# A three-block transformer kernel: the changes of sub-layer reordered, operands moved to equal addresses modulo 512, and another block order in the second-last weight unit

## The reference

```python
# first block, each with its own shift, scale, gate: x = x + c*(1 + gate) * rms_norm(f(h), post)
h = rms_norm(x, pre) * (1 + scale) + shift
f = swiglu, then hybrid_mixer (spatial gating beside forgetting attention), then swiglu
# second block: x = x + c * rmsnorm(f(rmsnorm(x, pre)), post)
f = swiglu, then hybrid_mixer_2 (RWKV-7 recurrence beside a convolution), then swiglu
# third block, twice, no post norm: x = x + f(rms_norm_3(x, g))
f = mixer (sparse attention beside differential attention), then swiglu
# at the end
return rms_norm_3(x, g_final)
```

## Time and profile before

| | |
|---|---|
| median of 3 runs | 3654.48 us (3650.88 to 3655.13) |
| the profiled execution, its own time | 3657.05 us |
| its span from first to last instruction | 3655.3 us |
| TensorE busy with matmuls | 3482.2 us (95%) |
| VectorE busy | 1837.7 us (50%) |
| ScalarE busy | 1152.5 us (32%) |
| moved by DMA | 330.29 MB, mean 90 GB/s |

### The profile page before, as it was taken

The page is one execution under the profiler, slowest core; times in us unless marked ns, Lnnn a source line. Parts: engine busy times, 40 slices in busy tenths (PEclk is TensorE's granted clock), DMA queues, the critical chain, the costliest instruction groups (busy, mean ns, idle before and its releaser), DMA issues.

```text
span 3655.3 us, 47516 instructions
## 1 busy us (share of the span) xinstructions
PE 3482.2 (95%) x19430; PEld 2770.4 (76%) x19436; DVE 1837.7 (50%) x2690; ACT 1152.5 (32%) x1728; POOL 162.7 (4%) x136
## 2 busy tenths in 40 slices
PE   9999899899999999998799999999999999899999
PEld 7887776678887888767588888666888886578887
DVE  6667535522334223798742225796422358952233
ACT  2222434422223222442342224335322233442222
POOL 0000000000000000000000001330000022200000
PEclk7999999999999999999999999999999999999999
DMA  6455221122222222220022222110222221112222
GB/s 245 178 182 196 81 95 47 58 81 92 92 92 88 100 94 92 81 79 15 8 87 92 96 98 94 70 69 24 81 93 100 95 93 70 47 53 92 92 93 81
DMA packets 47846, 330.29 MB, mean 90 GB/s; under 512 B 5312, under 2 KB 5568, under 8 KB 9280
## 3 DMA queue, kind: packets, MB, share of 16 engines
q1 hardware_dynamic: 41216, 290.09, 22.0%
q0 software_dynamic: 6464, 37.80, 2.8%
HBM read 325.77 MB, written 2.10 MB: 90 GB/s over the span
## 4 chain that ended last, share of the span: by engine, by line
PE 81%; DVE 13%; ACT 3%; issue 1%; DMA 0%; SPq 0%; DVEq 0%; ACTq 0%
PE PS L2136 24%; PE PS L2138 24%; PE PS L2137 24%; DVE WL L2640 2%; PE PS L319 1%; DVE A L1148 1%; DVE M L1147 1%; ACT WH L2435 1%; PE PS L394 1%; DVE X L2775 1%; PE PS L376 1%; PE PS L324 1%; PE PS L1493 1%; PE PS L931 1%; DVE A L2748 1%
## 5 line engine op out<-in xcount | busy, mean ns | idle before, releaser
L2640 DVE TENSOR_TENSOR WL<-RAW,WH 128x2048 fp32r<-128x2048 f32 x264 | 613.7, 2324 | 309.0 <-ACT WH L2435 308.6
L2136 PE MATMUL PS<-EH,WH 128*128 128x512 f32 (+1 forms) x1536 | 584.4, 380 | 28.9 <-DVE EL L2806 11.5
L2136 PE MATMUL PS<-HH,WH 128*128 128x512 f32 (+1 forms) x1456 | 556.0, 382 | 47.7 <-DVE HL L2806 23.4
L2137 PE MATMUL PS<-EL,WH 128*128 128x512 f32 (+1 forms) x1536 | 581.1, 378 | 0.0
L2138 PE MATMUL PS<-EH,WL 128*128 128x512 f32 (+1 forms) x1536 | 580.9, 378 | 0.0
L2435 ACT ACTIVATE WH<-RAW 128x2048 fp32r<-128x2048 f32 x264 | 503.9, 1909 | 191.6 <-PE PS L2138 183.5
L2137 PE MATMUL PS<-HL,WH 128*128 128x512 f32 (+1 forms) x1456 | 546.8, 376 | 0.0
L2138 PE MATMUL PS<-HH,WL 128*128 128x512 f32 (+1 forms) x1456 | 546.2, 375 | 0.0
L2679 DVE TENSOR_TENSOR A<-SG,PS 128x512 f32 (+1 forms) x132 | 90.7, 687 | 807.6 <-ACT SG L2565 807.6
L2565 ACT ACTIVATE SG<-PS 128x512 f32<-128x512 f32 x132 | 78.8, 597 | 1099.3 <-PE PS L2138 1099.3
L2136 PE MATMUL PS<-WH,AH 128*128 128x512 f32 x1056 | 417.7, 396 | 0.3 <-DVE CV L2868 0.3
(11 more groups left out here) (417 smaller groups left out, 3798.8 us busy)
## 6 DMA issues: line engine op xcount, KB each, us to landing
RAW<-in_w SPq DMA_DIRECT2D x264, 1024.0 KB, 4.8
E<-in_ada POOLq DMA_DIRECT2D x28, 1024.0 KB, 5.0
E<-in_ada SPq DMA_DIRECT2D x4, 1024.0 KB, 11.7
G<-in_ada SPq DMA_DIRECT2D x4, 1024.0 KB, 20.4
X<-in_x SPq DMA_DIRECT2D x1, 2048.0 KB, 13.9
X<-in_xn POOLq DMA_DIRECT2D x1, 2048.0 KB, 11.5
out_x<-A SPq DMA_DIRECT2D x4, 512.0 KB, 2.8
R<-in_row_ffn_post POOLq DMA_DIRECT2D x4, 256.0 KB, 3.1
```

The costliest lines, as they stand in the source:

```text
L2136: nc.tensor.matmul(out, wh, xh, start=start, stop=False)
L2137: nc.tensor.matmul(out, wh, xl, start=False, stop=False)
L2640: nc.vector.tensor_tensor(WL[:, w % 2, :], RAW[:, w % 2, :], WH[:, w % 2, :].bitcast(F32), ALU.subtract).then_inc(w_lo, 1)
```

## The change

It has four edits.

1. The spacer `LINE` is 40 floats long instead of 8, so everything behind it (EH, E, HH, G, AH, AL, ST and the smaller tensors) starts 128 bytes later in each partition: at 128 modulo 512, like X, WH, WL, A and ONES.
2. `leave`: the blocks of the second-last unit go 3, 2, 0, 1 instead of 3, 0, 1, 2, among those of the last unit.
3. ScalarE and VectorE take their steps at a change of sub-layer in another order: the high and low halves of tokens 0 to 255 come before the additions of blocks 2 and 3 to X, and the scaling of tokens 2 and 3 moves from VectorE to ScalarE (`scaled`), with a semaphore `root_ready`.
4. The Newton step takes two operations behind the root instead of three (four after a post norm); the factor -0.5 goes into the mean. `square_out(i)` waits for the squares of the block before.

```diff
-        sb("LINE", [P, 8])
+        sb("LINE", [P, 40])
...
                 one(0, 3)
+                one(0, 2)
                 one(0, 0)
                 second_arrives()
                 one(1, 0)
-                one(0, 1)
+                one(0, 1).then_inc(w_used, 1)
                 one(1, 1)
-                one(0, 2).then_inc(w_used, 1)
                 one(1, 2)
...
                 def square_out(i):
+                    if i:
+                        act.wait_ge(sqh_done, t("sqh") + 2 * i)
...
+                def scaled(i):
+                    act.wait_ge(root_ready, t.add("root_ready"))
+                    nc.scalar.activation(HG[:, i, :], XT[:, i, :], ACT.Copy, scale=stat(i, 6)).then_inc(xs_done, 1)
+
+                for i in (0, 1):
+                    if post:
+                        square_out(i)
+                        root_out(i)
+                    square_in(i)
...
+                    split(last_w)
+                    if post:
+                        square_out(2)
+                    for n in range(4):
+                        hi(n)
+                    if post:
+                        square_out(3)
+                    else:
+                        square_in(2)
+                    split(last_w + 1)
+                    for n in range(4, KD):
+                        hi(n)
+                    if post:
+                        root_out(2)
+                        root_out(3)
+                        square_in(2)
+                    else:
+                        square_in(3)
+                    scaled(2)
+                    if post:
+                        square_in(3)
+                    scaled(3)
                     for n in range(KD, 2 * KD):
                         hi(n)
...
+                def newton(i, r):
+
+                    dve.wait_ge(root_begun, t.add("roots"))
+                    chain(nc.vector.tensor_scalar(stat(i, 5), r, r, stat(i, 4), ALU.mult, ALU.mult))
+                    return nc.vector.tensor_scalar(stat(i, 6), stat(i, 5), 1.5, r, ALU.add, ALU.mult)
...
-                    dve.wait_ge(root_begun, t.add("roots"))
-                    chain(nc.vector.scalar_tensor_tensor(stat(i, 4), stat(i, 0), 1.0 / D, stat(i, 2), ALU.mult, ALU.add))
-                    i_[0] = i
-                    root = newton(stat(i, 4), stat(i, 3))
+                    chain(nc.vector.scalar_tensor_tensor(stat(i, 4), stat(i, 0), 1.0, stat(i, 1), ALU.mult, ALU.add))
+                    chain(nc.vector.tensor_scalar(stat(i, 4), stat(i, 4), -0.5 / D, -0.5 * EPS, ALU.mult, ALU.add))
+                    chain(newton(i, stat(i, 3)))
...
                     dve.wait_ge(sqx_done, t("sqx") + i + 1)
-                    chain(nc.vector.tensor_scalar(stat(i, 10), stat(i, 8), 1.0 / D, EPS, ALU.mult, ALU.add))
-                    dve.wait_ge(root_begun, t.add("roots"))
-                    i_[0] = i
-                    root = newton(stat(i, 10), stat(i, 9))
+                    chain(nc.vector.tensor_scalar(stat(i, 4), stat(i, 8), -0.5 / D, -0.5 * EPS, ALU.mult, ALU.add))
+                    root = newton(i, stat(i, 9))
+                    if onward and i >= 2:
+                        root.then_inc(root_ready, 1)
+                        return
+                    chain(root)
...
+                    leaves = gained if post else add_out
                     split(last_w)
+                    leaves(2)
+                    for n in range(4):
+                        lo(n)
+                    leaves(3)
+                    for n in range(4, KD):
+                        lo(n)
+                    if not post:
+                        normed(2)
+                    split(last_w + 1)
                     if post:
                         add_out(2)
...
+                        add_out(3)
+                        normed(2)
                     normed(3)
                     for n in range(KD, 2 * KD):
                         lo(n)
```

More of the change, by code:

```diff
@@ L190, in build_program @@
         sqh_done, hg_done, sqx_done, xs_done, turned = (sem(n) for n in ("sqh_done", "hg_done", "sqx_done", "xs_done", "turned"))
-        root_begun, y_shifted = sem("root_begun"), sem("y_shifted")
+        root_begun, root_ready, y_shifted = sem("root_begun"), sem("root_ready"), sem("y_shifted")
         xn_loaded, gains_loaded, gains_made, gains_ready = (sem(n) for n in ("xn_loaded", "gains_loaded", "gains_made", "gains_ready"))
@@ L2520, in boundary @@
                 else:
[L2521 to L2524, removed]
+                    split(last_w)
[3 more added lines that the diff above has]
+                        hi(n)
                     if post:
                         square_out(3)
-                        root_out(3)
[L2528 to L2532, removed]
+                    else:
[5 more added lines that the diff above has]
+                        root_out(2)
+                        root_out(3)
+                        square_in(2)
+                    else:
+                        square_in(3)
+                    scaled(2)
                     if post:
-                        square_in(2)
-                    square_in(3)
+                        square_in(3)
+                    scaled(3)
                     for n in range(KD, 2 * KD):
@@ L2774, in add_out @@
                     dve.wait_ge(hg_done, t("hg") + 2 * i + 2)
-                    nc.vector.scalar_tensor_tensor(XT[:, i, :], HG[:, i, :], root, XT[:, i, :], ALU.mult, ALU.add).then_inc(x_done, 1)
+                    nc.vector.scalar_tensor_tensor(XT[:, i, :], HG[:, i, :], stat(i, 6), XT[:, i, :], ALU.mult, ALU.add).then_inc(x_done, 1)
                 def normed(i):
                     dve.wait_ge(sqx_done, t("sqx") + i + 1)
-                    chain(nc.vector.tensor_scalar(stat(i, 10), stat(i, 8), 1.0 / D, EPS, ALU.mult, ALU.add))
-                    dve.wait_ge(root_begun, t.add("roots"))
-                    i_[0] = i
-                    root = newton(stat(i, 10), stat(i, 9))
+                    chain(nc.vector.tensor_scalar(stat(i, 4), stat(i, 8), -0.5 / D, -0.5 * EPS, ALU.mult, ALU.add))
[4 more added lines that the diff above has]
+                    chain(root)
                     dve.wait_ge(x_done, t("x") + i + 1)
                     if onward:
-                        nc.vector.tensor_scalar(HG[:, i, :], XT[:, i, :], root, None, ALU.mult).then_inc(xs_done, 1)
+                        nc.vector.tensor_scalar(HG[:, i, :], XT[:, i, :], stat(i, 6), None, ALU.mult).then_inc(xs_done, 1)
                         return
@@ L2788, in normed @@
                     for c in range(2):
-                        nc.vector.scalar_tensor_tensor(HG[:, i, c * S:(c + 1) * S], XT[:, i, c * S:(c + 1) * S], root, GAINS[s][c],
+                        nc.vector.scalar_tensor_tensor(HG[:, i, c * S:(c + 1) * S], XT[:, i, c * S:(c + 1) * S], stat(i, 6), GAINS[s][c],
                                                        ALU.mult, ALU.mult).then_inc(out_ready, 1)
@@ L2813, in boundary @@
                     normed(i)
-                if post:
-                    gained(2)
-                else:
+                if not onward:
                     add_out(2)
-                if not onward:
                     add_out(3)
@@ L2822, in boundary @@
                 else:
+                    leaves = gained if post else add_out
                     split(last_w)
+                    leaves(2)
[7 more added lines that the diff above has]
+                    split(last_w + 1)
                     if post:
                         add_out(2)
[L2826 to L2830, removed]
-                        add_out(3)
[L2832 to L2839, removed]
+                        add_out(3)
+                        normed(2)
                     normed(3)
```

## The result

| | before | changed |
|---|---|---|
| median of the runs, on the same chip | 3654.81 us (3650.88 to 3658.02, 4 runs) | 3601.06 us (3599.19 to 3605.64, 4 runs) |
| ratio, 95% interval | | 0.9855 [0.9838, 0.9872] |
| the profiled execution: its time, its span | 3657.05, 3655.3 us | 3600.26, 3598.6 us |
| TensorE busy with matmuls | 3482.2 us | 3416.8 us |

The kernel is faster by 53.8 us, 1.5%. The forecast was 3660.2 and the sign no change or slower, so it was wrong. What came is its first rival, that equal addresses raise the pace. That 3601.06 still lies inside the outer range of 3600 to 3680, by 1 us, is no merit of the forecast: its own range was 3652 to 3668.

A forecast was written before the change was run, and what follows sets the result against it. TensorE's matmul pace and waits were taken as the bound (busy 3482.2 of 3655.3 us); 1.6 - 2.0 + 5.1 + 1.0 = +5.7 us on the median 3654.48 gave 3660.2, own range 3652 to 3668, outer range 3600 to 3680.

The forecast's parts named there:

- first rival: Three-product matmuls on TensorE: equal addresses raise the pace; chance 0.28, much of it on small gains.
- Equal addresses: Three-products, operands 0 instead of 128 bytes apart modulo 512: pace stays 0.233 us, the edit priced at nothing.
- (a): Gate-up and down units: the distance has opposite signs, yet the pace is the same 0.233 us.
- (b): Matmuls of 512 and 256 columns: the loss goes with the columns, 20 and 11 ns over the estimate.
- (c): Plain float32 matmul at equal addresses, A on ONES: 0.43 us a row, compared with the three-product.
- The order of leaving: Second-last unit's blocks: blocks 0 and 1 complete 2.8 us later each, the turn of tokens 1 1.4 us later.
- With post: Four changes of sub-layer with post norm, without shift: turn of tokens 3 later by 0.4 us each, +1.6.
- With shift: First two changes of sub-layer: turn of tokens 3 earlier by 1.1 and 0.9 us, -2.0.
- second rival: The clock: waits before the turns of tokens 2 and 3 bring half rate behind them at six changes; chance 0.19.
- Without post: Three changes of sub-layer without post norm: VectorE's second low split ends late for TensorE, +1.7 us each, +5.1.
- The end: Kernel's end: block 1 arrives 2.8 us later, the last scaling ends at 3653.3 instead of 3652.27, +1.0.
- Rival 3: Three-product matmuls: equal addresses cost time; chance 0.09.

The follow-up runs named there:

- dist_256: Changed kernel with LINE of 104 columns instead of 40, so EH, HH and AH begin 256 bytes from WH mod 512; 3601.4 us.
- dist_64: Changed kernel with LINE of 56 columns instead of 40, so EH, HH and AH begin 64 bytes past WH mod 512; 3641.51 us.
- dist_192: Changed kernel with LINE of 88 columns instead of 40, so EH, HH and AH begin 192 bytes past WH; 3648.66 us.
- dist_32: Changed kernel with LINE of 48 columns instead of 40, so EH, HH and AH begin 32 bytes past WH mod 512; 3665.59 us.
- order_only: Changed kernel with the spacer back at 8 floats; reorder, leave order and shorter Newton steps stay; 3659.62 us, ratio 1.0014.
- old_leave: Changed kernel with the block order of the second-last unit put back to 3, 0, 1, 2; 3585.8 us, ratio 0.9813.
- old_leave_nopost: As old_leave, with the three changes of sub-layer without post norm also back in the earlier ScalarE and VectorE order; 3580.49 us, ratio 0.9798.

## Why the prediction was wrong, step by step

**Equal addresses** is the step that failed. It priced the edit at nothing. No run shows the "rate of the moving side" that this price rests on; what the runs show is that the same spacer alone takes 57.9 us off (`addr_only`), and that the pace changes with the place of the moving operand against the stationary one, 226.8 to 234.3 ns in the table above. I had three readings for the price. (a) That both signs of the distance have the same pace, 0.233. In `dist_256` the pace is 226.9 and 226.8 ns, that of distance 0. With such a period of 256 bytes, 128 ahead and 128 behind are the same place, so the two kinds of unit were one sample and not two; with the spacers of `dist_64` and `dist_192` the two signs do differ, 229.1 against 233.3 and 229.5 against 233.3. (b) That the loss goes with the columns. At clock 0.50 the matmuls of 512 columns start 427 ns apart and those of 256 columns 213: (1108.97 - 1107.69) / 6 = 0.213 us in the earlier trace rows. Half of that, 213 and 107 ns, is my estimate of what they would take at clock 1.00 if the rate of columns were all that set the pace. The kernel before lies 20 ns above it at 512 columns (0.233) and 11 at 256, (1126.12 - 1125.06) / 9 = 0.118 us in the earlier trace rows. I took this for the whole loss. At equal addresses what is left doesn't grow with the columns: TensorE in the changed kernel, a stretch at full clock of the half-width products, against the 0.118 of the earlier trace rows:

```profile
1110.22 0.28 PE L2136 MATMUL PS<-HH,WH 128*128 128x256 f32 x1
1110.34 0.28 PE L2137 MATMUL PS<-HL,WH 128*128 128x256 f32 x1
...
1111.06 0.28 PE L2137 MATMUL PS<-HL,WH 128*128 128x256 f32 x1
```

(1111.06 - 1110.22) / 7 = 0.120, 13 ns above the estimate of 107, and 226.9 is some 14 above that of 213. So the half of the 20 ns that I found at 256 columns said nothing of what equality would do at 512: it takes 6 ns off the wide matmuls and adds 1 to the narrow ones (118.7 to 119.7 as means). Nor are the 13 to 14 ns a fixed price of every matmul. At 256 columns `dist_192` has 115.4 and `dist_32` and `dist_64` have 117.2, all faster than equality. The half-width stretch of one change of sub-layer with EH moving, first in the changed kernel, then in `dist_192` (the counts take in the two or three matmuls that reach into the stretch from ahead of it):

```profile
2547.20:2557.20 10.00, 10.00 (x86) 10.00 (x85) 4.90 (x9) 5.36 (x8) 0.00 (x0) 1.00 0.00 0
2578.50:2588.50 10.00, 10.00 (x91) 10.00 (x90) 5.17 (x8) 5.29 (x8) 0.00 (x0) 1.00 0.00 0
```

What the remainder is made of stays open.

(c) The plain float32 matmul at equal addresses, A on ONES: 1.72 / 4 = 0.43 us a row. I compared it with the three-product and set it aside as a bound. It is none: a norm over 1024 channels issues eight of these matmuls, one for each 128 channels, and the trace has 16 rows for it (the first norm stands in the chain as `17.34 9.41 PE PS L2181 x16`), so 0.43 us is half a matmul, and no row shows what in it answers to one matmul of a three-product. What equal addresses bring is read from the runs alone: 233.1 to 226.9, 6.2 of the 20 ns, and some 14 stay. The best mean of a kernel here is 226.9.

**The order of leaving** was right in its sizes. The turn of tokens 1 was to be 4.99 us behind that of tokens 0 and the first product 9.43. In `order_only`, which has the addresses that the forecast reckoned with, they are 5.05 and 9.44 (1095.01, 1100.06 and 1104.45); in the changed kernel 5.26 and 9.65. The forecast netted two halves of opposite sign: the new order with the shorter Newton steps gains, and the block order gives it back, some 12.3 us at the old addresses.

**With post:** the turn of tokens 3 was to be 0.4 us later. In `order_only` it is 0.2 later (25.00 against 24.77, from the turn of tokens 0), and the four changes together are 1.2 us longer. The 25.18 of the changed kernel is no test of it: `addr_only`, with nothing reordered, has 25.12. The wait ahead of the turn of tokens 2 is 1.08 us in the changed kernel and 0.71 in `order_only`, not 2.5, because the stretch ahead of it takes longer: 11.0 us from the first product (12.12 - 1.08), where the forecast's times left 9.7.

**With shift:** -1.1 and -0.9 were forecast for the turn of tokens 3. In `order_only` it is 1.0 us earlier in the first change (29.17 against 30.13) and 0.3 in the second (29.63 against 29.96). At the end of the half-width work `order_only` stands 0.7 us later than before in the first change and 0.3 earlier in the second. So in the first one 1.6 us are lost behind the turn of tokens 3, and there the clock is at half rate, which the forecast had named as a sign of being wrong. The stretch behind its turn of tokens 3, in `order_only`, with the granted clock as the third column from the end:

```profile
466.90:473.60 6.70, 6.53 (x27) 5.63 (x26) 3.58 (x11) 0.23 (x1) 2.13 (x4) 0.50 0.22 54
```

and the same place in the kernel before:

```profile
470.40:477.20 6.80, 5.05 (x31) 3.92 (x31) 5.16 (x14) 1.16 (x3) 1.28 (x3) 1.00 0.03 4
```

Clock 0.50, where it was 1.00. It begins 5.9 us behind the turn of tokens 3 at 461.04. The changed kernel has it at the same place (461.20 to 468.00, clock 0.50). The second rival was that the waits before the turns of tokens 2 and 3 bring half rate behind them in each of the six changes. Half rate stands there in this one, not in all of them. That the waits before the two turns cause it isn't shown: in this change of `order_only` there is none before the turn of tokens 2 and 0.90 us before that of tokens 3. And `addr_only`, with nothing reordered and no wait before either turn, has half rate there too, though for less time; its turn of tokens 3 is at 460.44:

```profile
470.00:473.40 3.40, 3.40 (x18) 3.40 (x17) 0.01 (x1) 0.00 (x0) 2.13 (x4) 0.50 0.59 182
```

**Without post:** +1.7 each was forecast. The three differences at the end of the half-width work in `order_only` are 1.7, 1.5 and 1.6, and the run without that part is 5.3 us faster. The changed kernel's TensorE in the first of these changes shows the two waits that stand for it (forecast 2 and 1.3 us):

```profile
2534.77 0.39 PE L2136 MATMUL PS<-EH,WH 128*128 128x256 f32 x1 [1.46 <-DVE EL L2810]
2538.80 0.35 PE L2136 MATMUL PS<-EH,WH 128*128 128x256 f32 x1 [0.91 <-issue]
```

**The end:** the last scaling was to be 1.0 us later. From the start of the last matmul to its start it is 4.91 us before, 5.97 in `order_only`, 4.64 in `old_leave`: +1.1.

**The sum**, +5.7, met +5.1 between the medians of `order_only` and before (interval 1.8 to 8.4 us). Read from the one profile of `order_only`, against that of before, its terms are 1.2 with post (forecast 1.6), 0.35 with shift (-2.0), 4.8 without post (5.1) and 1.1 at the end (1.0), 7.4 in all (this execution took 6.9 us more than that of before). Only the term with shift is off by more than 0.5 us.

Rival 3, that equal addresses cost time, is refuted by `addr_only`: 57.9 us less.

## What to carry to other kernels

Where TensorE's pace is the bound and its matmuls start further apart than half of what they take at clock 0.50 (233 ns against 213 here), try where the operands begin: here a spacer of 128 bytes is worth more than every reorder around it (58 us against 16), and its effect can be read in one stretch without a wait. For 512-column matmuls of such a three-product keep every moving operand at 0 modulo 256 from the stationary ones, the low halves too (226.9 ns against 229.1 to 234.3 at the other distances here); at 256 columns equality was not the best place here (0.120 us against 0.115 in `dist_192`). Two readings that agree are one if the quantity may be periodic; and a part that "only" brings something forward by one block should be run apart from the rest of its change, since 16 us of gain and 15 of loss look like next to nothing together.

## What the runs showed that I had not expected

- The mean pace of the 512-column matmuls hangs on the distance of their operands' starts modulo 256 bytes, with a sign: 226.9 ns at 0, 229 to 229.5 at +64, 233 to 233.3 at -64, +32, -32, 128 and +96, 234.3 at -96.
- At 256 columns the same edit gains nothing: 0.119 us before, 0.120 after. Another place does: 0.115 with the operands 192 bytes apart.
- At clock 0.50 the distance costs nothing: single intervals of 512 columns are 426 to 427 ns in `order_only` and in `addr_only` alike.
- The mean clock differs between the kernels: it is 0.980 to 0.983 in the runs of `old_leave` and `old_leave_nopost`, 0.975 to 0.978 in those of `addr_only` and the changed kernel, and 0.976 to 0.980 in the runs of the kernel before beside them. What of the gains is the clock's isn't shown.
